# First rows of the sorted tokens made with the one-hot matrix as weights, and the sorted tiles turned after the first expert's second pass

## The chip, the core and the metric

The kernel runs on one core of a Trainium2 chip. A core has TensorE for matrix products and for turning (transposing) tiles, VectorE, ScalarE and GpSimd for everything element by element, and SyncE (SP), which here only issues DMA transfers. The metric is the device time of one execution in microseconds (us), the median of several. All data is f32.

## The reference, cut to what matters

One layer of a diffusion backbone: two token mixers, a projection, and a mixture of experts. The change lies in the last part. There are 384 tokens of 1024 values, 16 experts and two experts for each token, so 768 pairs.

```
g = argmax(group scores);  _, loc = top_k(scores in group g, 2)
expert = g * 4 + loc                     # two experts of each token
gates = sum(one_hot(expert, 16) * w)
hg = einsum('td,edf->tef', h, w_gate);  hu = einsum('td,edf->tef', h, w_up)
act = silu(hg) * hu * gates
out = einsum('tef,efd->td', act, w_down)
```

Each expert has three matrices of 2 MB: gate and up (1024 by 512) and down (512 by 1024).

## The kernel before

Every engine has its own program, written out by hand and tied to the others by semaphores; an engine works through its program in order.

**Routing and sorting.** VectorE computes for each pair its place in a list sorted by expert (`pos_u`), for each expert its count `n_i` and offset `off_i`. GpSimd scatters the rows of `h2` to `sorted_tokens` in memory (line 1762), SP brings them back as six tiles `hsr` of 128 rows (line 392), TensorE turns each tile in two halves of four turnings (`sorted_columns`, line 697), and ScalarE and VectorE copy the halves to `hTs`, which holds all sorted tokens with the 1024 values on the partitions (lines 1022 and 1511). The banks of PSUM alternate between tiles, so that tile t waits for the copies of tile t-2. Because that round trip through memory takes long, the first 64 rows are made directly: `places` is a 0/1 matrix (token, row 0 to 63), and line 774 multiplies h2 with it.

**An expert.** It works in passes of 64 rows. For a pass VectorE stages 64 columns of `hTs` into `xs` (`stage_x`, line 1516). TensorE forms gate and up (`gate_up`, line 712), 16 products whose weights are 64 columns of `xs`, each streaming 512 columns of the expert's matrices into one half of the partitions. ScalarE takes silu (line 1017), VectorE multiplies (line 1521), TensorE turns the result (line 735), VectorE copies it (`turn_over`, line 1526), TensorE multiplies with the down matrix (`down`, line 725). ScalarE evacuates (line 1033) and issues two stores to `sorted_outputs` (line 1037). The down product of a pass comes after the gate and up step of the next pass, except for every third expert (j = 2), where it comes first. Passes two to six run only if the count asks for them (`expert_rest`, branches on n); otherwise `skipped` raises the semaphores (line 744 is its own of TensorE). With these inputs experts 0, 3 and 15 have two passes, expert 2 three, all others one: 21 in all. The expert loops are hardware loops: 5 rounds of three experts on TensorE, 7 of two on ScalarE, 15 of one on VectorE.

**Order at the start.** After line 774 and the first gate and up step TensorE turns the one-hot tiles of the last expert (line 781), sorted tile 0, `hidden`, then tiles 1 to 5, and only then enters the loop with expert 0's second pass. VectorE copies six tiles and then enters its loop.

**Weights.** There are three sets of buffers. Set 2 lies where h2, `hsr` and the routing's small tables are, so expert 2 is loaded (lines 372 and 376) only after all six tiles are turned (`hs_ready` at 12). Sets are refilled from expert 3 on, gate and up when the expert that had the set has done its last gate and up step, down when its last down product is done (`reload`).

**The end.** Expert 15's outputs don't go through memory. GpSimd gathers the other outputs (line 1771), ScalarE weighs them (line 1086), VectorE joins them (lines 1606 to 1610).

## Time and profile before

| | us |
|---|---|
| three timed runs | 578.71, 580.58, 581.12 |
| their median | 580.58 |
| profiled execution | 576.9 |
| its span, first to last instruction | 575.1 |
| TensorE busy in it | 487.0 |

The page of the profile gives busy time by engine; the timeline gives each group of instructions with its start, its length and, in brackets, how long the engine was idle ahead of it and who released it. TensorE's clock has two levels, 2.4 GHz (shown as 1.00) and 1.2 GHz (0.50). TensorE has an f32 product in the trace as two records, a turning as one.

### The profile page before, as it was taken

The numbers are of one execution on the slowest core, as the hardware profiler recorded it, in microseconds if no ns is written. First come the engines' busy times: TensorE is split into PE (matmuls) and PEld (weight loads), VectorE is DVE, ScalarE is ACT, GpSimd is POOL, SyncE is SP. The second block draws the span as 40 slices with busy tenths as digits, with TensorE's granted clock in tenths as the row PEclk, the third lists the DMA queues.
The fourth block names the chain that finished last, engine by engine and source line by source line (L and its number), as shares of the span: only waits on it lengthen the run. The fifth ranks groups of instructions, "written<-read, shape, count | busy, mean of one in ns | idle before, by whom it ended". The sixth has DMA issues, their size and how long they took to land. (4 is left out here: it accounts for less than half of the span.)

```text
span 575.1 us, 8706 instructions
## 1 busy us (share of the span) xinstructions
PE 487.0 (85%) x3246; PEld 238.8 (42%) x3247; DVE 226.6 (39%) x542; ACT 146.7 (26%) x281; POOL 109.3 (19%) x185
## 2 busy tenths in 40 slices
PE   2779979999787999969799997898797798797873
PEld 1225668564686544656523332232232232232221
DVE  2689977999843105573400010100000000000086
ACT  3546873710367201420300110000000000001043
POOL 3000514888911061023000000000000000000341
PEclk9987999999888999975989999998998899898898
DMA  8990050856699920218999959399999999999732
GB/s 293 377 391 6 15 188 12 303 211 229 215 387 403 410 94 0 111 71 308 425 422 421 425 199 369 123 376 425 426 429 423 419 426 421 424 421 419 233 125 109
DMA packets 38149, 165.13 MB, mean 287 GB/s; under 512 B 2760, under 2 KB 3528, under 8 KB 32352
## 3 DMA queue, kind: packets, MB, share of 16 engines
q1 hardware_dynamic: 31408, 146.32, 64.3%
q10 hardware_dynamic: 4288, 10.33, 4.7%
q0 software_dynamic: 2416, 7.98, 3.7%
q8 instruction: 24, 0.39, 0.3%
q14 instruction: 13, 0.11, 0.1%
HBM read 153.28 MB, written 11.34 MB: 286 GB/s over the span
## 5 line engine op out<-in xcount | busy, mean ns | idle before, releaser
L712 PE MATMUL psum<-arena 128*64 128x512 f32 x672 | 159.6, 630 | 18.8 <-DVE arena L1516 12.8
L712 PEld LDWEIGHTS psum<-arena 128*64 128x64 f32 x672 | 52.3, 145 | 115.1 <-issue 107.1
L725 PE MATMUL psum<-arena 128*64 128x512 f32 x336 | 81.0, 626 | 17.4 <-ACTq L1044 14.4
L1521 DVE TENSOR_TENSOR arena<-arena,psum 128x256 f32<-128x256 f32 x21 | 8.8, 421 | 186.0 <-ACT arena L1017 186.0
L1771 POOL DMA_INDIRECT arena<-sorted_outputs,src_u x6 | 5.7, 955 | 277.7 <-DMA sorted_outputs<-arena 276.2
L725 PEld LDWEIGHTS psum<-arena 128*64 128x64 f32 x336 | 26.4, 144 | 65.0 <-issue 65.0
L1017 ACT ACTIVATE arena<-psum 128x256 f32<-128x256 f32 x21 | 8.1, 384 | 149.7 <-PE psum L712 149.7
L641 PE MATMUL psum<-arena 128*128 128x512 f32 x96 | 41.5, 592 | 0.0
L641 PEld LDWEIGHTS psum<-arena 128*128 128x128 f32 x96 | 18.2, 190 | 22.3 <-issue 22.0
L505 PE MATMUL psum<-arena 128*128 128x388 f32 x64 | 24.8, 537 | 1.1 <-ACT arena L880 1.1
L1033 ACT ACTIVATE arena<-psum 128x512 f32<-128x512 f32 x19 | 11.3, 597 | 49.6 <-PE psum L725 48.3
L463 PE MATMUL psum<-arena 128*2 128x512 f32 x64 | 17.5, 699 | 7.6 <-DMA arena<-in_w_mod 7.6
L1516 DVE COPY arena<-arena 128x512 f32 x20 | 8.6, 428 | 35.8 <-DVEq L1534 24.8
L863 ACT ACTIVATE arena<-arena 128x512 f32<-128x512 f32 x32 | 20.8, 715 | 7.1 <-DVE arena L1248 7.1
L513 PE MATMUL psum<-arena 128*128 128x388 f32 x64 | 21.1, 491 | 0.0
L592 PE MATMUL psum<-arena 128*128 128x512 f32 x48 | 20.9, 594 | 0.0
L448 PE MATMUL psum<-arena 128*2 128x128 f32 x512 | 17.7, 296 | 3.5 <-DMA arena<-in_w_mod 3.5
L1723 POOL TENSOR_TENSOR arena<-arena 128x64 f32<-128x64 f32 x32 | 14.9, 465 | 22.2 <-DVEq L1339 19.8
L448 PEld LDWEIGHTS psum<-arena 128*2 128x2 f32 x512 | 14.1, 91 | 6.3 <-issue 5.0
L505 PEld LDWEIGHTS psum<-arena 128*128 128x128 f32 x64 | 12.7, 207 | 9.2 <-issue 3.2
L1725 POOL TENSOR_TENSOR arena<-arena 128x64 f32<-128x64 f32 x32 | 15.2, 476 | 2.5
L513 PEld LDWEIGHTS psum<-arena 128*128 128x128 f32 x64 | 12.1, 190 | 8.5
(315 smaller groups left out, 642.3 us busy)
## 6 DMA issues: line engine op xcount, KB each, us to landing
arena<-in_w_gate SPq DMA_DIRECT2D x16, 2048.0 KB, 16.2
arena<-in_w_up SPq DMA_DIRECT2D x16, 2048.0 KB, 21.1
arena<-in_w_down SPq DMA_DIRECT2D x16, 2048.0 KB, 18.0
arena<-in_w_mod SPq DMA_DIRECT2D x12, 2048.0 KB, 15.2
arena<-in_w_in SPq DMA_DIRECT2D x3, 2048.0 KB, 19.5
sorted_outputs<-arena ACTq DMA_DIRECT2D x38, 128.0 KB, 7.5
arena<-in_w_out SPq DMA_DIRECT2D x2, 2048.0 KB, 14.5
arena<-modulation_rows ACTq DMA_DIRECT2D x3, 1024.0 KB, 10.6
```

Of the source, the lines that this page charges most:

```text
L448: last = mm(out[t], sil[:, k, :], w[:, k, t * P:t * P + P], start=(k == 0), stop=False)
L463: last = mm(bank[(4, 7)[c]][32 * t:32 * t + 2, :], sil[:, k, :], w[:, kk, t * D + c * 512:t * D + c * 512 + 512], start=(k == 0), stop=(k ...
L505: last = mm(bank[c][:, 0:TOK], w[:, k, c * P:(c + 1) * P], h1T[:, k, :], start=(k == 0), stop=(k == KD - 1))
L513: last = mm(out, w[:, k, c * P:(c + 1) * P], h1T[:, k, :], start=(k == 0), stop=(k == KD - 1))
L592: last = mm(bank[b][:, :], h1T[:, k, T0[t]:T0[t] + P], w[:, k, :], start=(k == 0), stop=(k == KD - 1))
L641: last = mm(bank[OUT_BANK[2 * t + h]][:, :], yT[:, k, T0[t]:T0[t] + P], wout[h][:, k, :], start=(k == 4), stop=(k == 3))
L712: last = mm(bank[0][HALF * t:HALF * t + HALF, :], xs[:, k, :], gu[:, :, k, t * 256:t * 256 + 256], start=(k == 0), stop=(k == KD - 1))
L725: last = mm(bank[4][HALF * h:HALF * h + HALF, :], hiddenT[:, s * P + t * HALF:s * P + t * HALF + HALF], dn[:, 2 * t + s, h * 512:h * 512 + ...
L863: last = A(out[:, :, 16 * g:16 * g + 16], made[i % 4], ACT.Copy, scale=side[:, c:c + 1])
L1033: A(ystage[:, y, :], bank[4][:, :], ACT.Copy).then_inc(S("evacuated"), 1)
L1723: p(G.tensor_tensor(pt1, prev, Tre, ALU.mult))
L1725: w(G.tensor_tensor(nxt, nxt, pt1, ALU.add))
```

## The change

- The first 64 rows: `places` becomes the weights (64 columns) and h2 streams, 256 columns a product, 12 products into halves of banks 2 and 5. ScalarE and VectorE copy 256 columns each to `first_rows`, TensorE turns four blocks, ScalarE and VectorE copy 256 columns each into `xs`.
- Sorted tile 0 is turned right after the first gate and up step, ahead of the one-hot tiles. Tiles 1 to 5 are turned after expert 0's second pass (`other_sorted_columns`), and ScalarE and VectorE copy them there. The banks of the tiles are a table now, `SORT_BANK`, without bank 4.
- `xs` has two sides. The first 64 rows of an expert go to side 0, the second 64 to side 1, and the latter are always staged, between `turn_over` and `multiply` (`to_next`), whether the expert has a second pass or not.
- SP loads expert 2's gate matrix once h2 and the small tables are free, and the up matrix once all tiles are turned.
- The first round of each expert loop is written out, and the loops start one round later.
- Semaphores are merged: `s_in` into `d_in`, `n2_in` into `ab_in`, `earlier_done` and `count_done` into `tri_done`; 64 columns fewer are cleared at the end of `hTs`. Those lines are not shown.

```diff
+READ = PAIRS + P + HALF
 SETS = 3
 PASSES = 6
 OUT_BANK = (4, 5, 6, 7, 0, 1)
+SORT_BANK = ((4, 5), (6, 7), (3, 5), (6, 7), (3, 5), (6, 7))
 UNIT = 4096
 EPS = 1e-6
...
-        hTs = view(F + 3072, KD, SORTED)
-        xs = view(F + 11264, KD, HALF)
+        hTs = view(F + 3072, KD, READ)
+        xs = view(F + 10752, 2, KD, HALF)
+        first_rows = view(F + 12544, 512)
         hiddenT = view(F + 11776, 256)
         sg = view(F + 12032, 256)
...
+            sp.wait_ge(S("tok_sent"), 16 * 6)
             for t in range(6):
-                if t == 0:
-                    sp.wait_ge(S("tok_sent"), 16 * 6)
                 sp.dma_start(hsr[:, t, :], hsd[t * P:(t + 1) * P, :]).then_inc(S(f"hs_in{t}"), 16)
             sp.wait_ge(S("unit_used"), 15)
             load_gate_up(1, 1)
             sp.wait_ge(S("yt_done"), 4)
             sp.wait_ge(S("modd_in5"), 16)
             load_down(1, 1)
+            sp.wait_ge(S("first_ready"), 1)
+            sp.wait_ge(S("onehots_done"), 1)
+            sp.wait_ge(S("pad_sent"), 48)
+            sp.dma_start(expert_weights(2)[0][:, 0], wg[:, 2, :, :]).then_inc(S("gu_in2"), 16)
             sp.wait_ge(S("hs_ready"), 12)
-            sp.wait_ge(S("pad_sent"), 48)
-            load_gate_up(2, 2)
+            sp.dma_start(expert_weights(2)[0][:, 1], wu[:, 2, :, :]).then_inc(S("gu_in2"), 16)
             load_down(2, 2)
...
                         k = 4 * h + kk
-                        last = tr(bank[4 + 2 * (t % 2) + h][:, kk * P:(kk + 1) * P],
+                        last = tr(bank[SORT_BANK[t][h]][:, kk * P:(kk + 1) * P],
                                   hsr[:, t, :].rearrange("p (q k) -> p k q", k=KD)[:, k, :], ident[:, :])
                     last.then_inc(S("hs_ready"), 1)
 
             pe.wait_ge(S("exp_done"), 1)
...
 
-            def expert_rest(j, e, use):
+            def other_sorted_columns():
+                pe.wait_ge(S("late_copied"), 2)
+                for t in range(1, 6):
+                    sorted_columns(t)
+                pe.wait_ge(S("hs_copied_a"), 6)
...
+
+            def expert_rest(j, e, use, is_first=False):
 
                 n = pe.value_load(n_i[0:1, bass.ds(e, 1)], min_val=0, max_val=NT * P)
                 with pe.If(n > HALF):
-                    gate_up(j, turn(1, e), None)
+                    gate_up(j, turn(1, e), None, 1)
                     down(j, use + 1, turn(1, e), turn(0, e))
                     transposes(turn(1, e))
+                    if is_first:
+                        other_sorted_columns()
                     with pe.If(n > P):
                         gate_up(j, turn(2, e), None)
...
                     with pe.Else():
                         skipped(e, 2)
                 with pe.Else():
+                    if is_first:
+                        other_sorted_columns()
                     skipped(e, 1)
 
             pe.sem_inc(S("downed"), 1)
             pe.wait_ge(S("placed"), 1)
-            for k in range(KD):
-                for t in range(NT):
-                    last = mm(bank[2][:, k * HALF:k * HALF + HALF],
-                              h2[:, t, :].rearrange("p (q k) -> p k q", k=KD)[:, k, :], places[:, t, :],
-                              start=(t == 0), stop=(t == NT - 1))
+            for t in range(NT):
+                for b in range(2):
+                    for h in range(2):
+                        k = 4 * h + 2 * b
+                        last = mm(bank[2 + 3 * b][HALF * h:HALF * h + HALF, 0:256], places[:, t, :],
+                                  h2[:, t, :].rearrange("p (q k) -> p k q", k=KD)[:, k:k + 2, :],
+                                  start=(t == 0), stop=(t == NT - 1))
+            last.then_inc(S("first_ready"), 1)
+            pe.wait_ge(S("first_held"), 2)
+            for kk in range(4):
+                last = tr(bank[1 - kk // 2][:, kk % 2 * P:kk % 2 * P + P], first_rows[:, kk * P:kk * P + P], ident[:, :])
             last.then_inc(S("first_sorted"), 1)
+            pe.wait_ge(S("first_staged"), 1)
             gate_up(0, 0, 1)
+            sorted_columns(0)
             pe.wait_ge(S("onehots_done"), 1)
             for i in range(2 * NT):
                 last = tr(bank[1 + 2 * (i // 4)][:, (i % 4) * P:(i % 4) * P + P], onehots[:, i // NT, i % NT, :],
                           ident[:, :])
             last.then_inc(S("late_ready"), 1)
-            sorted_columns(0)
             transposes(0)
-            for t in range(1, 6):
-                sorted_columns(t)
             pe.wait_ge(S("int_done"), 1)
-            pe.wait_ge(S("hs_copied_a"), 6)
-            pe.wait_ge(S("hs_copied_v"), 6)
-            with pe.Fori(0, 5) as i:
+
+            def three_experts(i):
                 for j in range(SETS):
                     e = i * SETS + j
-                    expert_rest(j, e, i)
+                    expert_rest(j, e, i, is_first=(isinstance(e, int) and e == 0))
                     if j == 2:
...
             row_half(7)
             A(warm[:, 0:1], epsc[:, :], ACT.Silu)
 
+            act.wait_ge(S("first_ready"), 1)
+            A(first_rows[:, 0:256], bank[2][:, 0:256], ACT.Copy).then_inc(S("first_held"), 1)
+            act.wait_ge(S("first_sorted"), 1)
+            A(xs[:, 0].rearrange("p (h k) j -> p h k j", h=2)[:, :, 0:2, :],
+              bank[1][:, 0:256].rearrange("p (k h j) -> p h k j", k=2, h=2), ACT.Copy).then_inc(S("first_staged"), 1)
+
...
+                act.wait_ge(S("gated"), at + 1)
+                A(sg[:, :], bank[0][:, 0:256], ACT.Silu).then_inc(S("silued"), 1)
+
+            def sorted_copy(t):
+                act.wait_ge(S("hs_ready"), 2 * t + 1)
+                A(hTs[:, 0:4, t * P:(t + 1) * P], bank[SORT_BANK[t][0]][:, :].rearrange("p (a b) -> p a b", a=4),
+                  ACT.Copy).then_inc(S("hs_copied_a"), 1)
...
                 n = act.value_load(n_i[0:1, bass.ds(e, 1)], min_val=0, max_val=NT * P)
                 A(warm[:, 0:1], epsc[:, :], ACT.Silu)
                 with act.If(n > HALF):
                     start = act.value_load(off_i[0:1, bass.ds(e, 1)], min_val=0, max_val=PAIRS - HALF)
                     gate(turn(1, e))
                     evacuate(2, turn(1, e), turn(0, e), start)
+                    if is_first:
+                        for t in range(1, 6):
+                            sorted_copy(t)
                     with act.If(n > P):
...
-                    gate(turn(0, i * 2 + y + 1))
-                    last_pass(i * 2 + y, y)
+                    e = i * 2 + y
+                    expert_rest(e, y, is_first=(isinstance(e, int) and e == 0))
+                    gate(turn(0, e + 1))
+                    last_pass(e, y)
+
+            two_experts(0)
+            with act.Fori(1, 7) as i:
+                two_experts(i)
...
                 dve.wait_ge(S("hs_ready"), 2 * t + 2)
                 cp(hTs[:, 4:8, t * P:(t + 1) * P],
-                   bank[5 + 2 * (t % 2)][:, :].rearrange("p (a b) -> p a b", a=4)).then_inc(S("hs_copied_v"), 1)
-
-            def stage_x(row):
-
-                cp(xs[:, :, :], hTs[:, :, bass.ds(row, HALF)]).then_inc(S("x_staged"), 1)
+                   bank[SORT_BANK[t][1]][:, :].rearrange("p (a b) -> p a b", a=4)).then_inc(S("hs_copied_v"), 1)
+
+            def stage_x(row, side=0):
+
+                cp(xs[:, side], hTs[:, :, bass.ds(row, HALF)]).then_inc(S("x_staged"), 1)
 
             def multiply(at):
...
 
             def skipped(e, done):
-                dve.wait_ge(S("x_staged"), turn(done, e))
+                dve.wait_ge(S("x_staged"), turn(max(done, 2), e))
                 dve.wait_ge(S("multiplied"), turn(done, e))
                 dve.wait_ge(S("turned"), turn(done, e))
-                dve.sem_inc(S("x_staged"), PASSES - done)
+                dve.sem_inc(S("x_staged"), PASSES - max(done, 2))
...
+            def other_sorted_copies():
+                for t in range(1, 6):
+                    sorted_copy(t)
+                dve.wait_ge(S("hs_copied_a"), 6)
+                dve.wait_ge(S("hs_copied_v"), 6)
+                dve.wait_ge(S("pad_done"), 1)
+
+            def expert_rest(e, is_first=False):
                 n = dve.value_load(n_i[0:1, bass.ds(e, 1)], min_val=0, max_val=NT * P)
                 with dve.If(n > HALF):
-                    s0 = dve.value_load(off_i[0:1, bass.ds(e, 1)], min_val=0, max_val=PAIRS - HALF)
-                    stage_x(s0 + HALF)
                     turn_over(turn(1, e))
                     multiply(turn(1, e))
+                    if is_first:
...
                 with dve.Else():
+                    if is_first:
+                        other_sorted_copies()
                     skipped(e, 1)
 
             dve.sem_inc(S("turned"), 1)
+            dve.wait_ge(S("first_ready"), 1)
+            cp(first_rows[:, 256:512], bank[5][:, 0:256]).then_inc(S("first_held"), 1)
...
+               bank[0][:, 0:256].rearrange("p (k h j) -> p h k j", k=2, h=2)).then_inc(S("x_staged"), 1)
             pos, start, from_held = g1.rearrange(flat)[:, 0:6], r2[:, 1, LAST:LAST + 1], r2[:, 0, 0:1]
             held_w, last_w, held_at = (g.rearrange(flat)[:, 0:6] for g in (g2, g3, g4))
             last_at = sel[:, 2, 0:6]
...
             multiply(0)
-            for t in range(6):
-                sorted_copy(t)
-            dve.wait_ge(S("hs_copied_a"), 6)
-            dve.wait_ge(S("hs_copied_v"), 6)
-            dve.wait_ge(S("pad_done"), 1)
-            with dve.Fori(0, NE - 1) as e:
-                expert_rest(e)
+            sorted_copy(0)
+            dve.wait_ge(S("hs_copied_a"), 1)
+            dve.wait_ge(S("hs_copied_v"), 1)
+            stage_x(HALF, 1)
+
+            def to_next(e):
                 nxt = dve.value_load(off_i[0:1, bass.ds(e + 1, 1)], min_val=0, max_val=PAIRS)
                 stage_x(nxt)
                 turn_over(turn(PASSES, e))
+                stage_x(nxt + HALF, 1)
                 multiply(turn(0, e + 1))
+
+            expert_rest(0, is_first=True)
+            to_next(0)
+            with dve.Fori(1, NE - 1) as e:
+                expert_rest(e)
+                to_next(e)
 
```

How it stands on each engine. TensorE, from the placing of the first rows (line 774) on. Before:

```order
L774 MATMUL psum<-arena 128x64 [waits exp_done,mrow_done,placed]
L774 MATMUL psum<-arena 128x64 x23
L712 MATMUL psum<-arena 64x512 [waits gu_in0,x_staged]
L712 MATMUL psum<-arena 64x512 x15
L781 MATMUL psum<-arena 128x128 [waits onehots_done]
L781 MATMUL psum<-arena 128x128 x5
L697 MATMUL psum<-arena 128x128 [waits hs_in0]
L697 MATMUL psum<-arena 128x128 x7
L735 MATMUL psum<-arena 128x128 [waits multiplied]
L735 MATMUL psum<-arena 128x128
L697 MATMUL psum<-arena 128x128 [waits hs_in1]
L697 MATMUL psum<-arena 128x128 x7
```

After (lines move: 791 and 797 are the new placing and its turnings, 716 is gate and up, 701 the sorted tiles, 804 the one-hot tiles, 739 `hidden`, 729 down):

```order
L791 MATMUL psum<-arena 64x256 [waits exp_done,mrow_done,placed]
L791 MATMUL psum<-arena 64x256 x11
L797 MATMUL psum<-arena 128x128 [waits first_held]
L797 MATMUL psum<-arena 128x128 x3
L716 MATMUL psum<-arena 64x512 [waits gu_in0,x_staged,first_staged]
L716 MATMUL psum<-arena 64x512 x15
L701 MATMUL psum<-arena 128x128 [waits hs_in0]
L701 MATMUL psum<-arena 128x128 x7
L804 MATMUL psum<-arena 128x128 [waits onehots_done]
L804 MATMUL psum<-arena 128x128 x5
L739 MATMUL psum<-arena 128x128 [waits multiplied]
L739 MATMUL psum<-arena 128x128
```

and further on:

```order
L760 TENSOR_LOAD n_i [waits int_done]
L760 ISA x2
L761 COMPARE_AND_BRANCH
L716 MATMUL psum<-arena 64x512 [waits x_staged]
L716 MATMUL psum<-arena 64x512 x15
L729 MATMUL psum<-arena 64x512 [waits turned,evacuated,dn_in0]
L729 MATMUL psum<-arena 64x512 x7
L739 MATMUL psum<-arena 128x128 [waits multiplied]
L739 MATMUL psum<-arena 128x128
L701 MATMUL psum<-arena 128x128 [waits hs_in1,late_copied]
L701 MATMUL psum<-arena 128x128 x7
L701 MATMUL psum<-arena 128x128 [waits hs_copied_a,hs_in2]
```

The 24 placing products have become 12 with four turnings, tile 0 stands ahead of the one-hot tiles, and a gate and up, a down and a turning step stand between `hidden` and tile 1.

VectorE, from the multiplication of the first pass on. Before (1511 copies a tile, 1516 stages):

```order
L1521 TENSOR_TENSOR arena<-arena,psum 128x256 [waits dve_own,silued]
L1511 COPY arena<-psum 128x4x128 [waits hs_ready] x6
L1594 UNCONDITIONAL_BRANCH [waits pad_done,hs_copied_v,hs_copied_a]
L1594 ISA
L1537 TENSOR_LOAD n_i
L1537 ISA x2
L1538 COMPARE_AND_BRANCH
L1539 REGISTER_ALU
L1539 TENSOR_LOAD off_i
L1539 ISA x2
L1516 ISA
L1516 COPY arena<-arena 128x512
```

After (1551 copies a tile, 1556 stages, 1566 is `turn_over`, 1561 `multiply`):

```order
L1561 TENSOR_TENSOR arena<-arena,psum 128x256 [waits dve_own,silued]
L1551 COPY arena<-psum 128x4x128 [waits hs_ready]
L1556 COPY arena<-arena 128x512 [waits hs_copied_v,hs_copied_a]
L1584 TENSOR_LOAD n_i
L1584 ISA x2
L1585 COMPARE_AND_BRANCH
L1566 COPY arena<-psum 128x256 [waits crossed]
L1561 TENSOR_TENSOR arena<-arena,psum 128x256 [waits silued]
L1551 COPY arena<-psum 128x4x128 [waits hs_ready] x5
L1590 COMPARE_AND_BRANCH [waits pad_done,hs_copied_v,hs_copied_a]
```

Five of six tile copies have moved behind the second pass's `turn_over` and `multiply`, and a staging copy stands right after tile 0's.

SP, at the load of expert 2. Before:

```order
L376 DMA arena<-in_w_down 128x4x1024 [waits modd_in5,yt_done]
L372 DMA arena<-in_w_gate 128x4096 [waits pad_sent,hs_ready]
L372 DMA arena<-in_w_up 128x4096
L376 DMA arena<-in_w_down 128x4x1024
L372 DMA arena<-in_w_gate 128x4096 [waits gated]
```

After:

```order
L379 DMA arena<-in_w_down 128x4x1024 [waits modd_in5,yt_done]
L403 DMA arena<-in_w_gate 128x4096 [waits pad_sent,onehots_done,first_ready]
L405 DMA arena<-in_w_up 128x4096 [waits hs_ready]
L379 DMA arena<-in_w_down 128x4x1024
L375 DMA arena<-in_w_gate 128x4096 [waits gated]
```

The gate matrix has lost the wait for `hs_ready`, the up matrix has it.

## Rows read from the trace of the kernel before

**Rows 1.** The page: span, and TensorE's busy time with its share and instructions

```profile
span 575.1 us, 8706 instructions
...
PE 487.0 (85%) x3246; PEld 238.8 (42%) x3247; DVE 226.6 (39%) x542; ACT 146.7 (26%) x281; POOL 109.3 (19%) x185
```

**Rows 2.** TensorE's timeline: start us, length us, line, [idle before <-releaser]

```profile
255.49 11.68 PE L774 MATMUL psum<-arena 128*128 128x64 f32 x48 [2.86 <-DVE arena L1487]
267.95 8.62 PE L712 MATMUL psum<-arena 128*64 128x512 f32 x32 [0.78 <-DVE arena L1563]
...
279.35 4.62 PE L697 MATMUL psum<-arena 128*128 128x128 f32 x40
287.30 8.78 PE L712 MATMUL psum<-arena 128*64 128x512 f32 x32 [3.34 <-DVE arena L1516]
...
300.87 7.09 PE L712 MATMUL psum<-arena 128*64 128x512 f32 x32 [0.98 <-PEq L744]
...
311.32 0.44 PE L735 MATMUL psum<-arena 128*128 128x128 f32 x2
312.42 7.09 PE L712 MATMUL psum<-arena 128*64 128x512 f32 x32 [0.67 <-PEq L744]
...
456.55 9.89 PE L712 MATMUL psum<-arena 128*64 128x512 f32 x32 [2.13 <-DVE arena L1516]
...
530.90 7.04 PE L712 MATMUL psum<-arena 128*64 128x512 f32 x32
```

**Rows 3.** Windows: stretch, length, busy by engine, TensorE's clock, DMA share, GB/s

```profile
255.50:267.00 11.50, 11.50 (x48) 11.48 (x48) 2.35 (x15) 0.00 (x0) 6.75 (x7) 0.50 0.73 285
276.60:287.30 10.70, 6.55 (x56) 6.17 (x57) 4.96 (x9) 4.83 (x10) 0.00 (x0) 1.00 0.99 419
...
289.00:291.00 2.00, 2.00 (x8) 0.67 (x6) 0.00 (x0) 0.00 (x0) 0.00 (x0) 0.50 1.11 455
```

**Rows 4.** Timeline of VectorE, and one row of ScalarE's DMA issues, at the start

```profile
258.11 0.15 DVE L1506 TENSOR_TENSOR wts<-arena 128x3 f32<-128x3 f32 x1
...
274.95 0.29 DVE L1586 TENSOR_TENSOR arena<-arena 128x128 f32<-128x128 f32 x1
...
284.00 0.69 DVE L1511 COPY arena<-psum 128x512 f32<-128x512 f32 x1 [0.20 <-PE psum L697]
286.82 0.43 DVE L1516 COPY arena<-arena 128x512 f32 x1 [2.12 <-issue]
287.16 0.42 DVE L1526 COPY arena<-psum 128x256 f32<-128x256 f32 x1
...
298.30 0.43 DVE L1516 COPY arena<-arena 128x512 f32 x1 [1.33 <-issue]
...
300.41 1.21 ACTq L1037 DMA_DIRECT2D sorted_outputs<-arena  x2
```

**Rows 5.** SP's issues and landings: tile 0, expert 2's up, expert 15's up

```profile
265.48 2.81 SPq L392 DMA_DIRECT2D arena<-sorted_tokens  x6
...
DMA to landing us min/median/max: 3.1/3.7/4.3
...
L372 SPq DMA_DIRECT2D arena<-in_w_up x1: 425/425/425, 284.4 to 284.4; - x1
...
DMA to landing us min/median/max: 18.2/18.2/18.2
...
L372 SPq DMA_DIRECT2D arena<-in_w_up x1: 454/454/454, 498.1 to 498.1; - x1
...
DMA to landing us min/median/max: 28.3/28.3/28.3
```

**Rows 6.** TensorE's timeline, second pass of expert 3

```profile
360.78 7.09 PE L712 MATMUL psum<-arena 128*64 128x512 f32 x32 [1.45 <-DVE arena L1516]
```

**Rows 7.** Timeline near the end, ScalarE's weighing and TensorE's last down

```profile
546.78 1.15 ACT L1086 ACTIVATE arena<-arena,wts 128x1024 f32<-128x1024 f32 x1 [8.42 <-DMA arena<-sorted_outputs,src_u]
...
556.38 3.65 PE L725 MATMUL psum<-arena 128*64 128x512 f32 x16 [3.01 <-DVE arena L1526]
```

62 lines of the change are left out of this document (29 added, 33 removed).

## The prediction, made before the changed kernel was run

> **What bounds the kernel now.** The page first: TensorE is busy 487.0 us of a span of 575.1 us [rows 1], so a change is worth what it takes off TensorE's own row of work or off a gap in it. I then read TensorE's timeline from the end of routing to expert 2. Placing the first rows takes 11.68 us from 255.49; expert 0's first gate and up products start at 267.95; the turning of tiles 1 to 5 is 4.62 us from 279.35; expert 0's second pass starts at 287.30 after 3.34 us of idle, and expert 1 at 300.87 [rows 2]. All of it is one chain, and the change rewrites it. The windows say at which clock: 0.50 of full speed (1.2 GHz) under the placing, 1.00 (2.4 GHz) under the turning, 0.50 again at 289 to 291 [rows 3]. The same rows show the DMA engines full (share 0.99 to 1.11, 419 to 455 GB/s) from about 276 on.
>
> In the trace one f32 product counts as two records (the 16 products of a gate and up step are x32), a turning as one.
>
> **Part 1: the first 64 rows.** Removed: 24 products whose weights are h2 (48 records, 11.68 us) and one copy of 512 columns. Added: 12 products with the 64 columns of `places` as weights and 256 columns of h2 streaming, then two copies of 256 columns, four turnings, two copies again. No row has that product shape. The nearest is the gate and up product, also 64 columns of weights with alternating halves, 512 streamed columns: 7.09/16 = 0.443 us at full clock [rows 2], so 0.22 for 256 columns, and 0.44 at half clock. Twelve are 2.7 us at full and 5.3 at half clock. If the halves didn't overlap it would be twice that, 10.6. I take 4.6: the stretch starts at half clock as now [rows 3], and the step at 267.95, which also begins there, took 8.62 instead of 7.09 [rows 2], an excess of 1.53 us, or about 3.1 us at half clock; the one at 456.55 lost 2.8 [rows 2]. The same excess of 1.5 to 2.6 us on 2.7 makes 4.2 to 5.3.
>
> So they end near 260.2. VectorE's integers and weights are through at 258.26 [rows 4] and no longer matter. A copy of 256 columns is 0.42 [rows 4], a turning 4.62/40 = 0.116 [rows 2], double at half clock; with about 0.05 for each hand-over and a last turning's 0.3 of latency: 0.45 + 0.7 + 0.5 = 1.65. The first gate and up step starts at 261.9 instead of 267.95, 6.1 us earlier. The two steps above were slow for 3.1 and 5.6 us from their start; 261.9 is 6.4 after 255.49, so I expect full clock here: 7.1 instead of 8.62, ending at 269.0 (before: 276.57).
>
> **Part 2: expert 0's second pass ahead of tiles 1 to 5.** Tile 0 must have come back from memory: issued at 265.48, landed 3.1 later, at 268.6 [rows 5]; that is no wait any more but close. Tile 0's eight turnings are 1.0, the one-hot tiles' six 0.7 (VectorE's chain for them now ends at 275.24 [rows 4]; it starts after the first staging, so about 6 earlier, at 269.4: no wait), the two of `hidden` 0.4. That is 271.2. Beside it ScalarE and VectorE copy tile 0 (0.69 [rows 4]) and VectorE stages the second rows (0.43 [rows 4]): 271.7. TensorE also loads n and branches, which the 0.67 us ahead of 312.42 [rows 2] bounds. The second pass starts at about 272.2 instead of 287.30. Its gate and up, down and turning last 311.32 + 0.44 - 300.87 = 10.9 [rows 2]: 283.1.
>
> Then come tiles 1 to 5. ScalarE first evacuates the first pass and issues two stores (1.21 us of issuing [rows 4]), so its first tile copy starts at 284.9, a microsecond after TensorE has tile 1 ready. The two bank pairs make TensorE wait for it; with 0.9 us a tile afterwards, the last VectorE copy ends at 289.0. VectorE then needs 1.33 us of branching and loading before a staging copy (the same skip, ahead of the copy at 298.30) where it now needs 2.12 (286.82) [rows 4], then 0.43. Expert 1 starts at 290.8 instead of 300.87: 10.1 us earlier. The wait of 3.34 ahead of the second pass is gone and one of about 2.7 stands ahead of expert 1.
>
> **Part 3: the weight loads.** SP now waits for `hs_ready` before the up matrix of set 2 only; the gate matrix goes out near 270. Up is issued when tile 5 is turned, at about 288.3 instead of 284.37. That costs nothing while the queue is full: before, up landed 18.2 after 284.37, at 302.6 [rows 5], behind expert 1's load and its own gate. The gate in front of it still lands at about 297.6, so up has 9 us of cover. But it doesn't land earlier either, and so 302.6 is a **floor** for expert 2, which starts at 312.42 now. Expert 2 would start 11.55 after expert 1, at 302.35. The gain there is capped at 9.8.
>
> A clock loss comes on top. The rows show the clock still at 1.00 while tiles were turned, then 0.50 from the start of the second pass, after 3.34 us of idle [rows 3]; that pass took 8.78 instead of 7.09 [rows 2]. Expert 1 now follows the turnings and 2.7 us of idle and may lose the same 1.7. Expert 2 starts at 302.6 without and 304.0 with the loss. I take 303.2, a **gain of 9.2**.
>
> On that the Trainium skill has a rule ("TensorE: Matmul & The Clock Gate", Part 4: PE-mode transpose): turnings don't count as TensorE work for its clock. By it the loss is certain and the gain 8.4; the rows in [rows 3] neither show nor deny it, since the clock held at 1.00 through the turnings.
>
> **Part 4: second rows always staged.** One more 0.43 us copy per expert on VectorE, between `turn_over` and `multiply`. `multiply` is the next thing queued behind it and waits for a gate and up step of 7.09 us [rows 2] anyway, so the copy is free; with that cover gone it would cost 0.43 for each of 15 experts, 6.5. It removes the copy and an offset load ahead of each second pass. Four experts have one. Expert 0 is in part 2; expert 2's had no wait; expert 3's waits 1.45 [rows 6]. TensorE's own load and branch stay, so of 1.45 I take 0.9 (bounds 0.3 and 1.45). Expert 15's second pass is not on the path: TensorE idles 3.01 ahead of the last down for VectorE's copy of line 1526, which stands behind joins of rows that ScalarE waited 8.42 for from memory [rows 7]. That chain starts from expert 14's stores. So 0.
>
> Unrolled first rounds and merged semaphores cost nothing on the path: the waits they merge come last already. I bound them by -0.5 and +0.5.
>
> **Sum.** 9.2 + 0.9 = 10.1 off the profiled execution's 576.9 us gives 566.8. The timed runs of before have a median of 580.6, 3.7 above it; with the same distance after, 570.5. From expert 4 on everything shifts alike, weights included, since their loads are issued by TensorE's progress. Expert 15's up matrix is issued at 498.11 and lands 28.3 later, at 526.4 [rows 5], 4.5 ahead of its use at 530.90 [rows 2]. So a luckier clock could give at most about 4.5 more.
>
> **Rivals.**
> *Streaming h2 with a stride is slow.* The 12 products read h2 eight elements apart. For it: no row streams such an operand. Against it: the turnings and the placing read the same stride as weights, and a strided turning at 0.116 us for 128 columns is one column every 0.9 ns, about the rate of half clock; so at that clock streaming should not slow down. If each read took double, the twelve cost 5 more; gain 10.1 - 5 = 5.1, **575.5**.
> *The same, at four times the time* is the case on the slower side: 12 x 1.76 = 21.1 us, 16.5 over my 4.6, so expert 2 starts 6.4 to 8.1 late and the result is near **586**. It turns from gain to loss once the twelve take about 14.7 us.
> The Trainium skill has this as a rule ("Advanced Engine Details and Errata", SBUF Cachelines): each access to a new 16-byte line costs extra, and eight f32 apart is a new line each time. The rows for strided weights don't bear it out, and it names no price.
> *The clock.* Gate and up steps at 8.6 to 9.9 instead of 7.09 stand all over the expert stage; all gaps move against each other. One or two more such losses, 1.7 each: gain 7, **573.6**. One or two fewer: gain 13, **567.6**, and no more than 4.5 because of the weights.
> *It doesn't move the bound:* expert 2's weights come later than 302.6 because the up matrix is issued later. It would need tile 5's turning to slip past 297.6, 9 us behind my account; with it the gain falls to 0 to 3, **579**.
>
> **How the numbers follow.** Forecast with its own range 568 to 573: 0.55. Clock against it (573 to 576): 0.15. Clock for it (565 to 568): 0.12. Double price of the stride (575 to 577): 0.07. Nearly no gain (577.7 to 583.5): 0.07. Slower by the stride: 0.04. A range of 565.5 to 576.5 leaves out less than 2 in 10. A measurement tells about 0.5% from no change: faster 0.89, same 0.07, slower 0.04.
>
> **What would show it.** Right: twelve products (24 records of 128x256) in 4 to 5.5 us; first gate and up near 262; second pass near 272; expert 1 near 291; expert 2 between 302.5 and 304.5, a wait for its weights possible; no 1.45 ahead of expert 3's second pass; the 3.01 near the end as before or longer. Wrong: the twelve over 7 us; TensorE waiting for tile 0's memory round trip; tile copies on ScalarE ending past 291; a longer wait for `multiplied` in any expert.

## The result, and the profile of the changed kernel

| | before | changed |
|---|---|---|
| median of 20 timed runs each, us | 579.01 | 581.86 |
| lowest to highest | 574.40 to 587.87 | 577.34 to 585.27 |
| ratio changed / before, 95% interval | | 1.0054 (1.0029 to 1.0079) |
| profiled execution, its span | 576.9, 575.1 | 584.98, 583.2 |
| granted clock over the span | 0.934 | 0.928 |

Forecast was 570.5 with 565.5 to 576.5. The changed kernel is not 10 us faster; it is some 3 us slower or, by the second measurement below (581.47, ratio 1.0017), about the same. Ratios leave out executions more than 1.5% above the fastest of the same kernel and medians don't, so for the three kernels of which many are left out (`one_copy` 7 of 12, `after_light` 4 of 12, `rows_staged_light` 3 of 6) the medians are the safer figure.

The page of the changed kernel, against [rows 1]. The last two rows are queues that carry program code; in the kernel before they read 24 packets (0.39 MB) and 13 (0.11 MB):

```profile
span 583.2 us, 8643 instructions
...
PE 483.2 (83%) x3226; PEld 234.4 (40%) x3227; DVE 232.7 (40%) x555; ACT 147.6 (25%) x283; POOL 110.1 (19%) x185
...
q8 instruction: 29, 0.48, 0.3%
q14 instruction: 15, 0.12, 0.1%
```

TensorE is busy 3.8 us less and the span is 8.1 us longer, so what was lost is idle time. Some of the 8.1 is not the change's: routing ends at 256.79 instead of 254.07, but also at 256.76 in a second profile of the kernel before. All positions below are therefore counted from the end of routing (VectorE's write of `pos_u`). From there to the end of the span it is 321.0 and 319.7 us in two profiles of before, 326.4 and 321.8 in two of the changed kernel.

TensorE's timeline of the changed kernel, against [rows 2]: start, length, line, and the idle time ahead:

```profile
258.21 5.76 PE L791 MATMUL psum<-arena 128*64 128x256 f32 x24 [2.85 <-DVE arena L1527]
...
265.72 7.09 PE L716 MATMUL psum<-arena 128*64 128x512 f32 x32 [0.56 <-ACT arena L1034]
...
275.21 7.09 PE L716 MATMUL psum<-arena 128*64 128x512 f32 x32 [0.44 <-DVE arena L1556]
...
288.55 2.94 PE L701 MATMUL psum<-arena 128*128 128x128 f32 x24 [0.66 <-ACT arena L1044]
298.63 9.98 PE L716 MATMUL psum<-arena 128*64 128x512 f32 x32 [7.14 <-issue]
```

The head of the chain does what it should: 24 records of the new shape in 5.76 us instead of 11.68, the first gate and up step at full clock (7.09), the second pass 14.8 us earlier. Then TensorE stands still for 7.14 us ahead of expert 1, released by nothing that the profile can name ("issue"), and the step that follows takes 9.98 us instead of 7.09, 2.9 us more, which is what half clock over its first 5.8 us would cost. Its operand had been staged long before, as VectorE's timeline shows (the copy of line 1556 ends at 294.27, 4.36 us before TensorE starts):

```profile
291.52 0.69 DVE L1551 COPY arena<-psum 128x512 f32<-128x512 f32 x1 [0.21 <-PE psum L701]
293.84 0.43 DVE L1556 COPY arena<-arena 128x512 f32 x1 [1.63 <-DVEq L1574]
```

What did arrive in that idle time is program code. The DMA view of the changed kernel from 296 to 297 us has one packet of the larger code queue among full queues of weights (the columns are packets, MB, share):

```profile
q1 hardware_dynamic: 22, 0.36, 84.0%
q8 instruction: 1, 0.02, 6.6%
```

Windows of TensorE around it (stretch, length, busy by engine, clock, DMA share, GB/s), against [rows 3]: the clock holds at 1.00 through the turnings, falls while TensorE is idle, and the step after the pause begins at 0.50 (from 304 to 308 us the clock is at 0.94):

```profile
286.00:293.00 7.00, 4.82 (x41) 4.46 (x40) 3.46 (x5) 3.25 (x6) 0.00 (x0) 1.00 1.00 393
293.00:298.60 5.60, 0.00 (x0) 0.00 (x1) 1.09 (x3) 0.00 (x0) 0.00 (x0) 0.61 1.05 441
298.70:304.00 5.30, 5.30 (x14) 1.78 (x16) 0.00 (x0) 0.00 (x0) 0.00 (x0) 0.50 0.99 416
```

Two more things happen late. TensorE, by then 3.5 us ahead of the kernel before (expert 12 at 230.5 against 234.0), waits for weights at experts 13 and 14, where before it waited for none, and goes cold (falls to the lower clock) once more. TensorE's timelines, first of the kernel before, then of the changed one:

```profile
498.59 8.78 PE L712 MATMUL psum<-arena 128*64 128x512 f32 x32 [2.14 <-DVE arena L1516]
...
511.84 7.09 PE L712 MATMUL psum<-arena 128*64 128x512 f32 x32 [0.67 <-PEq L744]
...
525.72 5.35 PE L725 MATMUL psum<-arena 128*64 128x512 f32 x16 [2.99 <-ACTq L1044]
```

```profile
498.08 8.78 PE L716 MATMUL psum<-arena 128*64 128x512 f32 x32 [2.39 <-DMA arena<-in_w_up]
...
513.66 9.98 PE L716 MATMUL psum<-arena 128*64 128x512 f32 x32 [3.00 <-DMA arena<-in_w_up]
...
530.71 6.56 PE L729 MATMUL psum<-arena 128*64 128x512 f32 x16 [3.27 <-ACTq L1074]
```

The wait at expert 13 stands where the kernel before waits 2.14 us for VectorE, so it costs only 0.25 us; the one at expert 14 costs 2.33.

And behind the last expert VectorE's last join takes 3.25 us instead of 1.23, with a GpSimd addition under way beside it, so that TensorE's wait of 3.01 us [rows 7] becomes 5.72. The timelines of VectorE and GpSimd before, then of VectorE, GpSimd and TensorE in the changed kernel:

```profile
554.68 1.23 DVE L1610 TENSOR_TENSOR arena<-arena 128x1024 f32<-128x1024 f32 x1
...
555.59 2.52 POOL L1777 TENSOR_TENSOR arena<-arena 128x1024 f32<-128x1024 f32 x1 [8.37 <-ACT arena L1086]
```

```profile
560.44 3.25 DVE L1668 TENSOR_TENSOR arena<-arena 128x1024 f32<-128x1024 f32 x1
...
560.16 2.44 POOL L1832 TENSOR_TENSOR arena<-arena 128x1024 f32<-128x1024 f32 x1 [7.11 <-ACT arena L1127]
562.67 3.21 POOL L1833 TENSOR_TENSOR arena<-arena 128x1024 f32<-128x1024 f32 x1
...
564.16 5.20 PE L729 MATMUL psum<-arena 128*64 128x512 f32 x16 [5.72 <-DVE arena L1566]
```

### The profile page after: what moved, and what is told of

Same layout as the page of the kernel before. It is cut to its first block and busy times, and to the rows that moved or that the text cites. A ratio compares the mean times of both kernels' runs of the same rounds, so it can differ in the third digit from the quotient of the medians.

```text
span 583.2 us, 8643 instructions
## 1 busy us (share of the span) xinstructions
PE 483.2 (83%) x3226; PEld 234.4 (40%) x3227; DVE 232.7 (40%) x555; ACT 147.6 (25%) x283; POOL 110.1 (19%) x185
## 5 line engine op out<-in xcount | busy, mean ns | idle before, releaser
L716 PE MATMUL psum<-arena 128*64 128x512 f32 x672 | 156.1, 619 | 22.8 <-issue 8.4
L729 PE MATMUL psum<-arena 128*64 128x512 f32 x336 | 87.2, 666 | 20.6 <-ACTq L1074 14.9
L716 PEld LDWEIGHTS psum<-arena 128*64 128x64 f32 x672 | 52.3, 142 | 115.5 <-issue 108.1
L729 PEld LDWEIGHTS psum<-arena 128*64 128x64 f32 x336 | 28.1, 153 | 72.9 <-issue 72.9
L645 PEld LDWEIGHTS psum<-arena 128*128 128x128 f32 x96 | 18.2, 190 | 22.3 <-issue 22.0
L1556 DVE COPY arena<-arena 128x512 f32 (+1 forms) x32 | 13.5, 422 | 31.8 <-DVEq L1574 28.6
L468 PE MATMUL psum<-arena 128*2 128x512 f32 x64 | 15.7, 638 | 9.9 <-DMA arena<-in_w_mod 9.9
L509 PEld LDWEIGHTS psum<-arena 128*128 128x128 f32 x64 | 12.5, 204 | 8.8 <-issue 2.7
L619 PE MATMUL psum<-arena 128*64 128x97 f32 x256 | 15.7, 272 | 0.0
```

Source lines behind the costliest of these rows:

```text
L468: last = mm(bank[(4, 7)[c]][32 * t:32 * t + 2, :], sil[:, k, :], w[:, kk, t * D + c * 512:t * D + c * 512 + 512], start=(k == 0), stop=(k ...
L509: last = mm(bank[c][:, 0:TOK], w[:, k, c * P:(c + 1) * P], h1T[:, k, :], start=(k == 0), stop=(k == KD - 1))
L619: last = mm(out[g], CA[:, ri, d * GP + gp, halves[g]], V[:, d, ri * GP + gp, d:d + NC], start=False, stop=(d == 1 and ri == 1))
L645: last = mm(bank[OUT_BANK[2 * t + h]][:, :], yT[:, k, T0[t]:T0[t] + P], wout[h][:, k, :], start=(k == 4), stop=(k == 3))
L716: last = mm(bank[0][HALF * t:HALF * t + HALF, :], xs[:, side, k, :], gu[:, :, k, t * 256:t * 256 + 256], start=(k == 0), stop=(k == KD - 1))
L729: last = mm(bank[4][HALF * h:HALF * h + HALF, :], hiddenT[:, s * P + t * HALF:s * P + t * HALF + HALF], dn[:, 2 * t + s, h * 512:h * 512 + ...
```

## The experiments

The table has all kernels. Positions are us from the end of routing, from one profile each: idle ahead of expert 1, start of expert 1's and 2's gate and up step, issue of expert 6's gate matrix, start of experts 14 and 15, and from expert 15's start to the end of the span. "Ratio" is to the kernel before, run beside it on the same chip. The groups ran at different times and not all on one chip: beside before2, after2, `one_copy` and `rows_only` the kernel before had a median of 580.49, beside `in_loop`, `rows_staged`, `before_light` and `after_light` 581.04, beside `in_loop_dead` and `rows_staged_again` 579.80, beside the other four 580.05.

| kernel | idle | exp. 1 | exp. 2 | load 6 | exp. 14 | exp. 15 | tail | median | ratio |
|---|---|---|---|---|---|---|---|---|---|
| before | 0.98 | 46.80 | 58.35 | 117.68 | 257.77 | 276.83 | 44.2 | 579.01 | |
| before2 | 0.88 | 46.71 | 58.26 | 117.43 | 257.65 | 274.97 | 44.8 | 579.83 | 0.9979 (0.9944 to 1.0014) |
| changed | 7.14 | 41.84 | 56.17 | 116.41 | 256.87 | 280.31 | 46.1 | 581.86 | 1.0054 (1.0029 to 1.0079) |
| after2 | 7.62 | 42.31 | 55.92 | 115.95 | 256.81 | 276.08 | 45.7 | 581.47 | 1.0017 (0.9984 to 1.0050) |
| one_copy | 2.92 | 37.60 | 50.59 | 110.55 | 254.41 | 273.76 | 47.8 | 581.83 | 0.9955 (0.9905 to 1.0006) |
| in_loop | 3.39 | 38.23 | 52.54 | 112.95 | 254.25 | 273.57 | 45.1 | 577.72 | 0.9975 (0.9945 to 1.0005) |
| in_loop_dead | 7.42 | 42.26 | 56.42 | 117.06 | 261.27 | 280.35 | 48.1 | 583.48 | 1.0058 (1.0024 to 1.0092) |
| unrolled_pe | 0.79 | 46.48 | 57.92 | 117.17 | 257.44 | 274.75 | 47.5 | 581.61 | 1.0074 (1.0038 to 1.0109) |
| rows_only | 0.97 | 42.33 | 53.88 | 114.62 | 254.19 | 276.35 | 48.2 | 575.74 | 0.9924 (0.9888 to 0.9961) |
| rows_staged | 0.90 | 39.50 | 51.05 | 111.48 | 250.81 | 268.10 | 47.3 | 574.25 | 0.9894 (0.9846 to 0.9941) |
| rows_staged_again | 0.89 | 39.47 | 51.02 | 109.78 | 249.31 | 269.77 | 48.3 | 572.69 | 0.9890 (0.9838 to 0.9942) |
| before_light | 0.89 | 49.16 | 60.71 | 121.38 | 256.98 | 276.27 | 44.1 | 580.76 | 1.0006 (0.9971 to 1.0040) |
| after_light | 7.34 | 42.03 | 55.84 | 115.97 | 256.84 | 276.05 | 46.3 | 579.13 | 0.9935 (0.9895 to 0.9976) |
| rows_staged_light | 0.89 | 40.10 | 51.65 | 110.40 | 250.65 | 270.11 | 45.3 | 571.58 | 0.9792 (0.9728 to 0.9856) |
| after_tail | 7.47 | 42.16 | 56.08 | 116.23 | 256.68 | 274.18 | 45.1 | 581.06 | 1.0012 (0.9974 to 1.0051) |
| rows_staged_tail | 0.89 | 39.46 | 51.02 | 109.71 | 250.48 | 269.65 | 45.4 | 574.67 | 0.9889 (0.9820 to 0.9958) |

### Are the long wait and the lost time there every time?

The kernel before and the changed kernel, unchanged, once more.

> The kernel of before once more, for a second trace and as a measure of what the timing resolves: ratio 0.997 to 1.003. The routing ended 2.7 us later in the trace of the changed kernel than in that of before; if that is chance, the two traces of before and the two of the changed kernel overlap there, if it comes from the change, they stand apart by about 2.7 us. Theory W: 154 to 157 us from expert 6's gate load to expert 15's up matrix landed.

> The changed kernel once more, for a second trace. Theory A (TensorE's own code arrives late): the idle time of 7.14 us ahead of expert 1's first step comes back, 6 to 8 us, with a fetch of instructions landing inside it, while expert 1's weights landed long before. Theory B (chance of one execution): 2.5 to 3.5 us this time. Theory W (the stream of weights sets the end): the time from the issue of expert 6's gate load to the landing of expert 15's up matrix is again 155 to 157 us, as in both traces so far (154.7 and 155.8).

The first loss is there again: 7.62 us idle ahead of expert 1, 9.25 us for its step, and TensorE ahead of before2 by only 2.3 us at expert 2 and 0.8 at expert 14. The waits for weights are not there in this profile: expert 13's step took 9.85 us, and so TensorE wasn't early enough to wait. The 9.98 at expert 14 came once only. From the issue of expert 6's gate to the landing of expert 15's up matrix it is 154.6 us in before2 and 155.8 in after2, as in the first two profiles.

### Where the code stands

`one_copy`: the turnings and copies of tiles 1 to 5 stand once, between two conditions, and not in both arms. The same was done on TensorE, ScalarE and VectorE; here TensorE's:

```diff
                     transposes(turn(1, e))
-                    if is_first:
-                        other_sorted_columns()
-                    with pe.If(n > P):
+                if is_first:
+                    other_sorted_columns()
+                with pe.If(n > HALF):
+                    with pe.If(n > P):
...
                 with pe.Else():
-                    if is_first:
-                        other_sorted_columns()
                     skipped(e, 1)
```

> The changed kernel with the turnings and copies of tiles 1 to 5 written once, between two branches on n, and not in both arms of one branch. Nothing else. Theory A (late code: TensorE jumps over 40 turnings of the arm that is not taken and over four passes): the idle time ahead of expert 1 falls from 7.1 to about 3, expert 1 has no or a shorter slow stretch, expert 2 starts 4 to 7 us earlier against the end of routing, and the time falls by 4 to 7 us against the changed kernel, to 0.5 to 0.8% below before. Rival (the idle time has another cause, such as expert 1's weights or the staging): it stays near 7 us and the time is that of the changed kernel.

The wait ahead of expert 1 is 2.92 us, against a forecast of 2.7 for it, and expert 2 is 5.6 us earlier than in the changed kernel. But the median, 581.83, did not follow, and the expected gain of 4 to 7 us on the changed kernel did not come. TensorE's timeline shows a new pause at expert 5's down, with code packets landing in the windows from 393 and from 399 us:

```profile
392.16 0.44 PE L739 MATMUL psum<-arena 128*128 128x128 f32 x2
397.22 5.94 PE L729 MATMUL psum<-arena 128*64 128x512 f32 x16 [4.62 <-DVE arena L1563]
```

VectorE's copy (line 1563), which TensorE waits for here, had itself waited 4.20 us for TensorE's own queue (line 748).

So I put the loops back as well. `in_loop` is the changed kernel with nothing unrolled; the tiles stand once, under a condition on the round (ScalarE and VectorE alike):

```diff
-                if is_first:
-                    other_sorted_columns()
+                if j == 0 and e is not LAST:
+                    with pe.If(use < 1):
+                        other_sorted_columns()
...
-            three_experts(0)
-            with pe.Fori(1, 5) as i:
+            with pe.Fori(0, 5) as i:
                 three_experts(i)
```

> The changed kernel with its three loops whole again as in the kernel before (nothing unrolled): the turnings and copies of tiles 1 to 5 stand once, inside the loops, under a condition that holds in the first round alone. Theory A (TensorE's program itself arrives late: the unrolled first round and the second copy of the 40 turnings put a long jump ahead of expert 1, and the loops' bodies are fetched a second time while the DMA engines are full): no wait over 3.5 us ahead of expert 1, expert 1's gate and up step 37 to 38.5 us after the end of routing (41.8 in the changed kernel), expert 2's at 49.5 to 51 (56.2), no packets of the instruction queues between experts 3 and 6, expert 4 at 110 to 112 (117.2), expert 6's load issued 6 to 8 us earlier than in the kernel before; time 571 to 576. Rival B (the idle time ahead of expert 1 belongs to the new order of tiles, copies and weights, wherever the code stands): expert 1 again at 41 to 42.5, time 580 to 583.

The wait is 3.39, the code queues are back at 24 and 13 packets, and the kernel is 3.8 to 4.1 us faster than the changed one by the medians, 2.4 to 4.6 by the ratios. Expert 1 stands where theory A put it (38.23); expert 2 does not (52.54 instead of 49.5 to 51), because expert 1's step took 9.84 us behind the wait: that clock loss belongs to the order of the work, not to the code. The time, 577.72, is 1.7 above the expected range, and still above the 576.5 up to which the prediction's own range goes. This left open whether the second copy or the unrolling made the long wait, so the copy alone was added back, never executed:

```diff
                 with pe.Else():
+                    if j == 0 and e is not LAST:
+                        with pe.If(n > P + HALF):
+                            for t in range(1, 6):
+                                sorted_columns(t)
                     skipped(e, 1)
```

> The changed kernel with whole loops (tiles 1 to 5 once, under the condition on the round), to which only a copy of the 40 turnings is added that is never executed: it stands in the arm that holds where an expert's rows don't need a second pass, behind a condition that never holds there, so that TensorE jumps over it ahead of expert 1 as in the changed kernel. Executed work is the same as without it (577.7; wait ahead of expert 1 3.39 us, its gate and up step 38.2 after the end of routing). Theory A (the jump over code that isn't loaded, while the DMA engines are full): the wait ahead of expert 1 grows to 6.5 to 7.6 us, its step stands at 41 to 42.5, an instruction packet lands in that wait; time 579 to 583. Rival B (the longer wait of the changed kernel comes with the unrolled round, not with the copy): 3.4 and 38.2 as without it, 577 to 578.5.

That settles the long wait. TensorE's timelines ahead of expert 1, first without the dead copy, then with it:

```profile
288.21 2.92 PE L701 MATMUL psum<-arena 128*128 128x128 f32 x24 [0.81 <-ACT arena L1043]
294.53 9.84 PE L716 MATMUL psum<-arena 128*64 128x512 f32 x32 [3.39 <-DVE arena L1553]
```

```profile
289.37 2.92 PE L701 MATMUL psum<-arena 128*128 128x128 f32 x24 [0.81 <-ACT arena L1047]
299.71 9.69 PE L716 MATMUL psum<-arena 128*64 128x512 f32 x32 [7.42 <-issue]
```

And VectorE's staging copy for expert 1, in the same order:

```profile
293.96 0.43 DVE L1553 COPY arena<-arena 128x512 f32 x1 [2.09 <-issue]
```

```profile
295.14 0.43 DVE L1557 COPY arena<-arena 128x512 f32 x1 [2.12 <-issue]
```

The executed work is the same in both, but for a comparison and a branch more where the arm is taken, and the staging copy starts 37.7 us after the end of routing in both. Without the dead copy TensorE starts at 38.2, with it at 42.3. A packet of the larger code queue lands in the window from 297 us, while TensorE is idle; in `in_loop` it lands in the window from 295, when TensorE has already started, and in the kernel before from 296, while TensorE works. Forty turnings that never run make the wait 4.0 us longer and the kernel 5.8 us slower by the medians (4.8 by the ratios), a little above the expected 583. How much of the 4.0 comes from the full queues is not shown: no run makes such a jump while they are empty.

`unrolled_pe` does the other half alone: the kernel before with TensorE's first round written out.

```diff
-            with pe.Fori(0, 5) as i:
+            def three_experts(i):
...
+            three_experts(0)
+            with pe.Fori(1, 5) as i:
+                three_experts(i)
```

> The kernel before with TensorE's first round of three experts written out ahead of a loop of four rounds, and nothing else. The prediction's Part 4: costs nothing on the path (within 0.5 us), 580 to 581. Theory A: the loop's body is first entered at expert 3, so its code is fetched while the DMA engines are full, one piece in about every expert from 3 to 6 (instruction packets between 345 and 400 us, none there in the kernel before); each can hold TensorE up by 0 to 4.6 us, so 0 to 4 us slower, 580 to 584, and the jump ahead of expert 1 is short, so no long wait there.

Its page has five code packets more on q8 (29), and the DMA view from 358 to 402 us, where that of the kernel before has none, shows where:

```profile
q8 instruction: 5, 0.08, 0.7%
```

The measured ratio is 1.0074, the medians of this comparison differ by 1.6 us (581.61 to 580.05). But in its profile no step up to expert 14 is late: it is 0.3 us ahead of the kernel before there, and the tail is longer by 3.3 us, 2.0 of it for the reason given under "The end". One trace of a cost there is. From the issue of expert 6's gate to the landing of expert 14's up matrix it takes 140.2 to 140.7 us in the five profiles with whole loads and TensorE's first round written out (changed, after2, `after_tail`, `one_copy`, `unrolled_pe`), and 139.2 to 139.4 in the eight with whole loops. Here TensorE waits 0.74 us at expert 14, and for that matrix. So the refetching shows in the packets and probably in 1 us of the weights' stream; that it makes up the measured 1.6 us is not shown. In `one_copy` they coincided with one 4.62-us pause.

### The parts that pay

`rows_only` is the kernel before with Part 1 of the change alone (ones as weights, and the merged semaphores that make room for its new ones). `rows_staged` has Part 4 too: `xs` with two sides, the second rows always copied. Loops, tile order and loads stay as before.

```diff
-            for k in range(KD):
-                for t in range(NT):
-                    last = mm(bank[2][:, k * HALF:k * HALF + HALF],
+            for t in range(NT):
+                for b in range(2):
+                    for h in range(2):
+                        k = 4 * h + 2 * b
+                        last = mm(bank[2 + 3 * b][HALF * h:HALF * h + HALF, 0:256], places[:, t, :],
...
                 turn_over(turn(PASSES, e))
+                stage_x(nxt + HALF, 1)
                 multiply(turn(0, e + 1))
```

> The kernel of before with the first part of the change alone: first 64 rows with the one-hot matrix as weights, the two rounds of copies, four turnings, and the merged semaphores that it needs. Tiles, staging and loops as before. Expected: the first gate and up step starts 5 us earlier against the end of routing, but the tiles then wait for their memory round trip and the second pass starts 4 to 6 us earlier; the time falls by 3 to 5 us (0.5 to 0.9%) if nothing else takes it back. Rival: expert 2's weights, loaded when all tiles are turned, and the weight stream behind take it back, same within 0.5%.

> The kernel before with the first 64 rows formed in the new way and the second rows always staged, loops whole, tiles 1 to 5 still turned ahead of expert 0's second pass. Prediction's Part 4: expert 3's wait of 1.45 us ahead of its second pass falls to 0.3 to 1, nothing else longer: 0.5 to 1 us faster than the kernel with the new first rows alone (575.7), so 574.5 to 575.5. Rival (the additional copy of 0.43 us per expert gets in the way of VectorE's row of work after all): up to 6.5 us slower than it, 577 to 582, with `multiplied` or `turned` arriving later in each expert.

> The fastest kernel so far once more, word for word: new first rows and second rows always staged on the kernel before, loops whole, tiles ahead of expert 0's second pass (574.25, ratio 0.9894 with 0.9846 to 0.9941 from six runs). If that holds: 573 to 576, ratio 0.985 to 0.993. If it was a lucky chip: 576 to 579.

Both are faster than either kernel, and `rows_staged` repeats: 574.25 and 572.69, ratios 0.9894 and 0.9890. It has expert 1 at 39.5 with tiles 1 to 5 still ahead of the second pass, only 1.3 us later than `in_loop` has it with the tiles behind, and expert 2 1.5 us earlier, since expert 1's step follows a short gap at full clock. The first run, 574.25, is a little below the 574.5 to 575.5 expected. Its TensorE timeline:

```profile
283.48 8.78 PE L713 MATMUL psum<-arena 128*64 128x512 f32 x32 [2.23 <-DVE arena L1528]
...
296.96 7.09 PE L713 MATMUL psum<-arena 128*64 128x512 f32 x32 [0.90 <-PEq L745]
```

The wait ahead of the second pass falls from 3.34 [rows 2] (3.35 in `rows_only`) to 2.23 by the staging alone, since VectorE's copy no longer stands behind a branch and a load.

`in_loop` has what `rows_staged` has, and besides it the new order of the tiles and of expert 2's loads, with the condition that this needs in the loops. It is 3.5 to 5.0 us slower by the medians, and the interval of its ratio, 0.9975 (0.9945 to 1.0005), lies just above those of both `rows_staged` runs. So the new order loses time of its own, with no second copy of any code. In the profiles it is 1.3 us ahead at expert 1, 1.5 behind at expert 2 (the step of 9.84 us) and 3.4 to 4.9 behind at expert 14; what loses the rest was not taken apart.

### Does the stream of weights set the end?

Three kernels load only half the bytes of each expert's weights from expert 6 on; all products are still made, half of them with weights of an earlier expert.

```diff
-                    sp.dma_start(gu[:, i], w[:, e, :, :]).then_inc(S(f"gu_in{j}"), 16)
+                    n = KD if e < 6 else KD // 2
+                    sp.dma_start(gu[:, i, 0:n], w[:, e, 0:n, :]).then_inc(S(f"gu_in{j}"), 16)
```

> The kernel before with only half of the bytes of each expert's three weight matrices loaded from expert 6 on (the other half of each buffer keeps the weights of an earlier expert; all products are still made). Theory W (from expert 6 on the continuous stream of weights paces TensorE): with half of the bytes the DMA engines have gaps, no wait for weights is left at experts 13 and 14, and the time falls only as far as TensorE itself waited: 0 to 3 us, 577.5 to 580.5, since here TensorE and the stream end within 1 us of each other. Rival (TensorE alone sets the time): the same within 1 us.

> The changed kernel with the same halved loads from expert 6 on. Theory W: the waits of 2.4 and 3.0 us for weights ahead of experts 13 and 14 and the cold steps of 9.9 us behind them go, and what the head gained (1.0 to 1.5 us at expert 6) reaches the end: 1 to 2 us faster than the kernel before with halved loads, where with whole loads it is 3 us slower, so 576 to 579. Rival T (the 3 us are lost behind the last expert, in the joins and last stores, whatever the weights do): again 2 to 3 us slower than the kernel before with halved loads, with the waits for weights gone.

> The kernel before with the new first rows and the second rows always staged, with only half of the bytes of each expert's weights loaded from expert 6 on (the other half of each buffer keeps earlier weights; all products are made). With whole loads it took 574.25, and its TensorE waited 3.40 and 3.03 us for weights ahead of experts 13 and 14. Theory W (the continuous stream of weights from expert 6 on sets the end once TensorE gains more than about 1 us): both waits go and the time falls by 3 to 7 us, to 567 to 571, where the same cut did nothing for the kernel before (1.0006). Rival (the waits only take the place of TensorE's own idle time and clock losses elsewhere): within 1 us of 574.25.

The cut does nothing that can be measured for the kernel before (1.0006). The changed kernel goes from 1.0017 to 1.0054 down to 0.9935; by the medians it is 1.9 us faster than the kernel before beside it (579.13 to 581.04) where it was 1.0 to 2.9 slower. For `rows_staged` the ratio falls from 0.9894 to 0.9792, but the intervals meet, and by the medians the lead over the kernel before goes from 6.8 and 7.1 us to 8.5, with six runs between 564.81 and 574.41 and a median just above the expected 567 to 571: a gain there is likely and not shown. The halved loads also leave the DMA engines free for stores and code, which these runs don't tell apart from the weights. The waits for weights at experts 13 and 14 are gone in both. TensorE's timeline of `rows_staged` at these two, whole and halved loads:

```profile
492.65 8.78 PE L713 MATMUL psum<-arena 128*64 128x512 f32 x32 [3.40 <-DMA arena<-in_w_up]
...
508.27 7.09 PE L713 MATMUL psum<-arena 128*64 128x512 f32 x32 [3.03 <-DMA arena<-in_w_up]
```

```profile
494.54 8.78 PE L715 MATMUL psum<-arena 128*64 128x512 f32 x32 [2.15 <-DVE arena L1530]
...
507.83 7.09 PE L715 MATMUL psum<-arena 128*64 128x512 f32 x32 [0.71 <-PEq L747]
```

What is gained lies in the timed runs. In the single profiles nothing is: expert 14 starts at 250.81 and 250.65 here, at 256.87 and 256.84 in the changed kernel, though the waits are gone; the profiled executions took 574.34 and 582.28 us, 2.8 and 3.2 more than the medians. Expert 14's up matrix lands 139.2 us after the issue of expert 6's gate in the kernel before, 140.4 in the changed one, 139.2 in `rows_staged`: the stream runs at its own pace from there, within 1.5 us in all thirteen profiles with whole loads. What the head moves that issue it can pass on (1.3 us in the changed kernel, 6.2 and 7.9 in `rows_staged`); what TensorE wins behind it can be stopped at expert 14. In three profiles of the changed kernel's code (changed, after2, `after_tail`) expert 12 is 3.5, 2.2 and 3.9 us ahead of the kernel before, expert 14 only 0.9, 1.0 and 1.1. In two of the three it was the wait for the weights that took this away, in after2 a step of 9.85 us.

### The end

Eight of fourteen profiled executions without the wait below have VectorE's last join at 3.24 to 3.37 us instead of 1.22 or 1.23: those in which GpSimd's first addition had started 0.04 to 0.34 us before it. In the six where GpSimd started later (in two of them by only 0.02 and 0.03 us) the join is short. `after_tail` and `rows_staged_tail` make GpSimd wait:

```diff
             pool.wait_ge(S("weighed"), 4)
             pool.wait_ge(S("g2_in"), 48)
+            pool.wait_ge(S("join_step"), 6)
```

> The changed kernel with one wait more: GpSimd begins its three joining operations only when VectorE has done its six. Theory L (VectorE and GpSimd don't work at the same time on these operands: where GpSimd's first operation starts before VectorE's last join, that join takes 3.25 instead of 1.23 us and the last down step of TensorE comes 2 us later; in the kernel before GpSimd happened to start after it): VectorE's last join takes 1.23 us, expert 15's start to the end of the span falls from 45.7 to 46.3 to 44 to 45, and the time by 0 to 2 us, to 579.5 to 581.5. Rival (the 3.25 us come from elsewhere, or GpSimd's later start makes the third tile's addition late): no gain, or up to 3 us slower.

> The kernel before with the new first rows, the second rows always staged, and GpSimd's joining operations behind VectorE's. Theory L: the 47.3 us from expert 15's start to the end of the span (44.2 in the kernel before; VectorE's last join 3.32 us) fall to 44 to 45.5, the time from 574.25 to 571.5 to 573.5. Rival: 574 or more, the third tile's addition waiting for GpSimd.

The join is short in both (1.22 and 1.23), the tail 45.1 (44 to 45 expected) and 45.4 (44 to 45.5 expected); the times are not measurably better (581.06; 574.67 with 0.9889, against 0.9894 and 0.9890 without). A wait of 2 us is gone from the trace, and the last down step is cold behind it all the same (6.14 us in `rows_staged_tail`). The second is above the 571.5 to 573.5 of theory L. So the mechanism is shown and its price is not: it is below what these runs can tell.

## Why the prediction was wrong

**Part 1, right in mechanism, 1.2 us too short.** I said 4.6 us within 4 to 5.5; 5.76 were measured. I let the clock rise after about 4 us, though [rows 3] has it at 0.50 under the placing for 11.5 us; in the changed kernel it is at 0.50 until 263 us, 4.8 us after the first product, and at 0.54 over the twelve. My own 5.3 for half clock was the value to take, and 0.4 to 0.8 us are left over it. The double and fourfold prices of the stride are refuted. The Trainium skill's rule on cachelines ("Advanced Engine Details and Errata", SBUF Cachelines) names no price; what these runs leave for one is at most those 0.4 to 0.8 us, and they don't show that they come from the stride. The first gate and up step came 4.95 us earlier instead of 6.1, at full clock (7.09), as forecast.

**Part 2, right up to the tiles and wrong behind them.** The second pass 14.8 us earlier (15.1 forecast), 7.09 us long; the last tile copy of VectorE ends 35.4 us after routing (34.9 by the prediction). Then the wait ahead of expert 1 was 7.14 instead of 2.7, and its step 9.98 instead of 7.09 to 8.8. Of the wait, 4.4 us come after the operand was staged, and `in_loop_dead` shows what they are: TensorE's own program, arriving late after a jump over code that is never executed. That it is late because the DMA queues are full fits the rows and was not tested by itself.

**The step that failed** is therefore the last line of Part 4, "unrolled first rounds and merged semaphores cost nothing on the path", bounded by 0.5 us. The diff showed both the second copy of the 40 turnings and the second copy of the rounds, and no rival was made of it: I read the code for what is executed, not for where it lies. It cost about 4 us at expert 1, and 3.8 to 5.8 us by the medians (changed against `in_loop`, `in_loop_dead` against `in_loop`). It is not the whole of the miss: `in_loop`, without that fault, gains 5.8 us at expert 2 and not 9.2, and at 577.72 it too lies outside 565.5 to 576.5.

**Part 3 never came into play.** The floor of 302.6 for expert 2 was right as a mechanism (up landed at 305.41, 48.6 us after routing), but TensorE came later than it, at 56.2. The gain at expert 2 was 2.2 instead of 9.2. The clock loss on which the Trainium skill's rule bore ("TensorE: Matmul & The Clock Gate", Part 4: turnings don't count for the clock) did come at expert 1: 9.98, 9.25, 8.63 and 9.84 us (changed, after2, `one_copy`, `in_loop`). By the windows the clock was still 1.00 during the turnings and fell in the pause behind them, so here, too, the rows don't tell the turnings' part from the pause's. I took half of 1.7 for it; it was 1.5 to 2.9, and a further 1.7 went at one of expert 2's down steps (5.35 us against 3.65).

**The sum** has a second fault, the other step that failed, in "from expert 4 on everything shifts alike, weights included" and "a luckier clock could give at most about 4.5 more". I had looked at expert 15's up matrix, 4.5 us ahead of its use. Expert 14's landed at 510.93 and was used at 511.84: 0.9 us. So whatever TensorE wins behind expert 6's loads counts for no more than that. It did win there: with the second rows always staged it lost the clock less often (three gate and up steps over 7.1 us in each profile of the changed kernel, five and six before), and 2.2 to 3.9 us gained by expert 12 came down to 0.9 to 1.1. And a gain in front of expert 6 doesn't pass whole: `in_loop` has 5.8 us at expert 2, 4.7 at expert 4, 3.5 at expert 14 and 2.3 at the end, with no wait for weights. The halved loads bear the limit out in the timed runs of the changed kernel.

**Part 4's staging** was under-sized: I took 0.9 us. Expert 3's wait fell from 1.45 [rows 6] to 0.67 in the changed kernel and 0.98 in `rows_staged`, and expert 0's second pass gained another 1.1 us of wait in the kernel that keeps the old order. It is part of 1.5 us by the medians from `rows_only` to `rows_staged`; the intervals of the two overlap.

**The tail** was called unmoved. It was 46.1, 45.7 and 46.3 us in the profiles of the changed order against 44.2, 44.8 and 44.1. Some of it is the short or long join, which a race of some 0.3 us between two engines decides; after2 has the short join and 45.7 all the same.

Together: 10.1 us forecast; 5.0 left at expert 1, 2.2 at expert 2, 1.3 at expert 4, 0.9 at expert 14, and behind that 4.4 us lost at expert 14 (4.1 by the clock, in this profile only) and 1.9 in the tail. Of the rivals, "it doesn't move the bound" (579) was nearest in size, but for another reason: expert 2's weights landed where forecast, and the mechanism that held TensorE up I hadn't named.

## What to carry over

When a diff writes code out twice or moves it into an arm, ask when that code is loaded and what the DMA queues are doing then; a condition inside the loop kept the loop's code loaded and cost nothing that shows. When a head is made faster, find the first transfer whose landing is less ahead of its use than the gain, for every user and not only for the last. And try the parts of a change by themselves: here two of them were worth 1.1%, the new order took about 0.8% of that back even with its code in one place, and writing the code out took the rest (0.4 to 0.8%).

## What was not expected of the hardware

- Code comes through the same DMA engines as data (29 packets of 16 KB on q8, 0.3% of their time). In a stretch with a DMA share of 1.0, forty turnings jumped over cost TensorE 4.0 us of wait; a loop entered for the first time in round two fetched its body again, five packets of 16 KB.
- VectorE and GpSimd did not work on their 128x1024 additions at the same time: 1.23 us became 3.24 to 3.37 when GpSimd was earlier, if only by 0.04 us, and two 128x512 products of VectorE took 5.22 us beside GpSimd in the kernel before, 3.43 in the two kernels where GpSimd waits.
- Streaming an operand with a step of eight f32 was nowhere near twice as slow: 24 records of 128x256 in 5.76 us at a clock of 0.54, where the gate and up step's rate at half clock gives 5.3 (an estimate).
